# Low weights of 24 feed-forward units made by an accumulating DMA in place of a VectorE subtraction

## The chip, the cores and the metric

The kernel runs on one core of a Trainium2 chip. The metric is the device time of one execution in microseconds, the median over the executions shown. TensorE (PE in the profile) does the matrix products, VectorE (DVE) and ScalarE (ACT) the elementwise work, GpSimd (POOL) little besides constants, and SyncE (SP) issues nearly all weight loads.

## What is computed

A trunk of two layers for 512 prompt frames and 32 sample frames, 544 tokens in all, with a model width of 1024. Around each mixer stand two feed-forward blocks, four in the kernel:

```python
def swiglu(x, w_gu, w_down):
    gate, up = jnp.split(x @ w_gu, 2, axis=-1)
    return (jax.nn.silu(gate) * up) @ w_down
...
def trunk(x, ssm0, conv0, gla0, hgrn0, p):
    ...
    for l in range(DEPTH):
        h = h + 0.5 * swiglu(rms_norm(h, p['norm_ffn1'][l]), p['ffn1_w_gu'][l], p['ffn1_w_down'][l])
        u = rms_norm(h, p['norm_mix'][l])
        ...
        h = h + m
        h = h + 0.5 * swiglu(rms_norm(h, p['norm_ffn2'][l]), p['ffn2_w_gu'][l], p['ffn2_w_down'][l])
```

The hidden width is 2816, that is 22 tiles of 128. Everything is float32.

## The kernel before, in words

**High and low parts.** TensorE is fed float32r operands, which hold fewer bits than float32. Each weight block and each activation is therefore split in two: a high part, the float32r copy, and a low part, the float32r copy of what is left. A product is then three matmuls: high by high, high by low activation, low weight by high activation.

**Units.** A unit is one output tile of 128 rows. Its weights are up to 8 blocks of 128x128 (768 or 1024 columns in a buffer). SyncE loads them into one of four buffers `raw` (`load`); ScalarE copies them to `whi[u % 2]` (`hi`); VectorE subtracts, `raw - whi`, into `wlo[u % 2]` (`lo`); TensorE then multiplies (`unit`, or `unit_rows` for some of its blocks; `row_products` is one block, six matmuls). ScalarE, VectorE, TensorE and SyncE each have an order of their own written out in the code; semaphores tie them: `raw_landed`, `hi_ready`, `lo_ready`, `unit_done`. Since `raw` and `wlo` are reused, SyncE waits with a load for the `lo` of the unit four before, and ScalarE waits with a `hi` for the end of the unit two before.

**The feed-forward blocks.** They are named l0f1, l0f2, l1f1 and l1f2. Each has 8 units for the first four hidden tiles, and then three groups of hidden tiles with 8, 6 and 8 tiles (`GROUPS`). In a group, the gate and up products of most tiles are made by seven partial products each (`product`, p1 to p7, with weights WH and WL); then comes the down projection of the group, 8 units whose block count is the group's tile count: `down0` (8 blocks), `down1` (6 blocks), `down2` (8 blocks).

**Where a down group begins.** TensorE's order is: the last p7 of the group, then blocks 0 and 1 of the first down unit u0, then p3 and p4 of the last hidden tile, then the other blocks of u0, then the units u0+1 to u0+7. TensorE waits for `lo_ready` of u0 before its first matmul, although the low weights are read only by the fifth. ScalarE's order there is: silu of the tile before the last, the copy after p6 of the last tile (`u2_copy`), `hi(u0)`, the copy after p7 (`u3_copy`), one `act_hi`, `hi(u0+1)`, `last_silu`. After that, at the end of each unit u0+j, comes the `hi` of unit u0+j+2. VectorE makes `lo(u0)` and `lo(u0+1)` in the same places, and `lo(u0+j+2)` after the residual of u0+j.

The memory `LR`, `SQ` and `ACC` (one row of 544 numbers each) is used at the ends of blocks and in the mixers, not in down0 and down1.

Of the kernel before, what the change touches and what calls it, by code (L numbers as in the profile page):

```python
# [6 lines left out]
FR = mybir.dt.float32r  # L7
I32 = mybir.dt.int32
ALU = mybir.AluOpType
# [3 lines left out]
P = 128  # L13
# [75 lines left out]
def build(nc, a, o):  # L89
# [3 lines left out]
    with ExitStack() as ctx:  # L93
        def sem(name):
            return ctx.enter_context(nc.semaphore(name))
# [26 lines left out]
        ACC = place("ACC", [T], w)  # L122
        SQ2 = LR
        assert 2 * T >= D
        ident = place("ident", [P], w)
# [123 lines left out]
        end_unit = plan[f"{FFNS[-1][0]}_down{len(GROUPS) - 1}"][0]  # L249

        def kept(u):

            return u >= end_unit + WHOLE
# [5 lines left out]
        def low_of(u):  # L259

            return KW[:, u - end_unit - WHOLE, 1] if kept(u) else wlo[u % 2]

# [86 lines left out]
        def tile(x, m):  # L349
# [5 lines left out]
            xh_ready xl_ready sq_ready acc_done ms_ready rs_ready gate_scaled silu_done act_made ah_ready al_ready  # L355
            lowrank_landed late_rows lb_exp small_landed masks_made row_placed first_tap conv_ready xc_ready z_scaled sz_ready
            dt_in dt_exp dt_plus dt_turned dt_made cum_made rows_psum rows_copied last_rows last_copied last_stored y_summed dct_psum b_turned bt_ready end_diff end_exp cb_psum cb_masked rows_stored lms_landed lm_landed ep_landed lms_ready st_turned lms_masked lm_exp ep_ready
            x_turned xd_made bx_psum hs_ready lm_ready y_psum y_read y_gated y_squared y_mean y_rstd
            y_weighted yh_ready yl_ready h0_psum h0_landed h0_ready hout_copied hout_stored scan_consts_made st_ready gk_psum pre_act forget_made clamped logs_made q_made g_taken far_placed att_ready last_done last_read b_ready e1_ready
# [3 lines left out]
            pair_high pair_low pair_sums product_done pair_copied c22_made parts_high parts_made front_scaled front_silu""".split()  # L363
# [3 lines left out]
        pair_landed = [sem(f"pair_landed{b}") for b in range(2)]  # L367
        y_stored = sem("y_stored")
        passed = {e: sem(f"waits_passed_{e}") for e in ("sp", "pe")}
# [25 lines left out]
        def _(sp):  # L395
            xp = a["x_prompt"].rearrange("b (c t) d -> t (b c) d", t=CH)
            def load(u, slot, src, k, n=P, dst=0):

                hold("sp", S["lo_ready"], u + 1)
                return sp.dma_start(raw[slot][:, 0:k, dst:dst + n], src)  # L400
# [97 lines left out]
            sp.dma_start(DROW[:, :], a["ssm_d"].broadcast_to([P, HA])).then_inc(S["small_landed"], 16)  # L498
            sp.wait_ge(S["late_rows"], 3)
            sp.dma_start(WGK[32:48, :], a["gla_w_gk"][0]).then_inc(S["gate_weights_landed"], 16)  # L500
# [18 lines left out]
            for b in range(2 * KT):  # L519
                col = (COL_XBC, COL_Z)[b % 2] + b // 2 * P  # L520
                load(u0 + b, (u0 + b) % 4, win[:, :, col:col + P], KT).then_inc(raw_landed[(u0 + b) % 4], 16)
                if b == 1:
                    sp.wait_ge(S["rows_stored"], 16)
                    sp.wait_ge(S["late_rows"], 2)
# [56 lines left out]
        def _(pool):  # L581
# [31 lines left out]
            pool.drain().then_inc(S["masks_made"], 1)  # L613

            def scan_consts(m):

                pool.memset(m["rm"][:, :], 1.0)
                pool.memset(m["att"][:, :, :], 0.0)
                pool.memset(m["ac"][:, :, :], 0.0)
                pool.memset(m["vw"][:, :, T:TPAD], 0.0)  # L620
                pool.memset(m["kd"][:, T:TPAD], 0.0)
                pool.memset(m["xl"][:, LV - 2, :], 0.0)
                pool.drain()
                pool.memset(m["rm"][:, 0:T:CH], 0.0)
                pool.drain().then_inc(S["scan_consts_made"], 1)

            pool.wait_ge(S["unit_done"], plan["ab_heads"][0] + CREDIT)
            states_out(pool)
            scan_consts(GM)
            pool.wait_ge(S["rs_ready"], 5)  # L630
            scan_consts(CM)


        @block.scalar
        def _(act):
# [19 lines left out]
            def run(name, evac, begun=False):  # L655
# [14 lines left out]
                for b in range(min(4, n)):  # L670
# [21 lines left out]
            def rms(e, name=None):  # L692

                logs_set()
                if e == 2:
                    act.wait_ge(S["late_rows"], 1)
                    A(LB[:, 1, :], LB[:, 0, :], ACT.Exp).then_inc(S["lb_exp"], 1)
# [90 lines left out]
            def ffn(f, e, name=None, final=False, after_first=None):  # L788
# [25 lines left out]
                for g, nf, ss in groups(f):  # L814
# [6 lines left out]
                    for s in ss:  # L821
# [659 lines left out]
        def _(dve):  # L1481
            TT, STT, TSC = dve.tensor_tensor, dve.scalar_tensor_tensor, dve.tensor_scalar

            def lo(u):

                k = unit_rows[u]
                dve.wait_ge(S["hi_ready"], u + 1)
                TT(low_of(u)[:, 0:k, :], raw[u % 4][:, 0:k, :],  # L1488
                   high_of(u)[:, 0:k, :].bitcast(F), ALU.subtract).then_inc(S["lo_ready"], 1)
# [332 lines left out]
            lo(2)  # L1822
            dve.wait_ge(S["masks_made"], 1)
            ffn(0, 1, begun=True)

            dve.wait_ge(S["early_vec"], 3)
            TT(LB[:, 0, :], vec[:, V_LB:V_LB + KT], vec[:, V_LB:V_LB + KT], ALU.subtract).then_inc(S["late_rows"], 1)
# [3 lines left out]
            dve.drain().then_inc(S["late_rows"], 1)  # L1831
            dve.memset(WGK[0:64, :], 0.0)
            dve.drain().then_inc(S["late_rows"], 1)
# [3 lines left out]
            dve.wait_ge(S["masks_made"], 1)  # L1837
            dve.memset(PM[:, 2, NC * HA:(NC + 1) * HA], 0.0)
# [267 lines left out]
            def heads(name, nh, m, g0, weights, first, t0):  # L2106
# [165 lines left out]
                if not gla:  # L2272
                    pre(0)
                    units(0, 2)
                dve.wait_ge(S["scan_consts_made"], first)
                cumulate(0)
# [198 lines left out]
            for j in range(KT):  # L2475
# [3 lines left out]
                lo(u0 + j + 2)  # L2479
            dve.wait_ge(S["lb_exp"], 1)  # L2480
            dve.reciprocal(LB[:, 2, :], LB[:, 1, :])
# [17 lines left out]
        def _(pe):  # L2499
# [44 lines left out]
            def unit_rows(ps, r0, r1, k, x, before=None):  # L2544

                if r0 == 0:
                    pe.wait_ge(S["lo_ready"], ps + 1 + CREDIT)
                    pe.wait_ge(S["pair_read"], ps - 1 + CREDIT)
# [650 lines left out]
```

## Time and profile before

| | |
|---|---|
| median of 2 runs | 2325.43 us (2325.21 to 2325.66) |
| span of the profiled execution, which is its own time | 2325.5 us |
| TensorE busy | 2294.0 us, 99% |
| VectorE busy | 1720.5 us, 74% |
| ScalarE busy | 1143.9 us, 49% |
| GpSimd busy | 14.4 us, 1% |
| packets of the main load queue, share of 16 DMA engines | 30.7% |

An engine that is busy 99% leaves little to gain by relieving another one. What matters is at which places TensorE's next work is ready only just in time.

### The profile page before, as it was taken

Reading aid. Unit: us, or ns where it says so; the run is one execution under the profiler, and the core shown is the slowest. Engines: PE = TensorE matmul, PEld = TensorE weight load, DVE = VectorE, ACT = ScalarE, POOL = GpSimd, SP = SyncE. Lnnn points to the kernel's source line nnn. Section 1 sums busy time; section 2 is a strip of 40 time slices with the busy share of each in tenths; the row PEclk is TensorE's granted clock in tenths of the full one; section 3 lists DMA queues with packets and bytes.
Section 4 is the critical chain, followed back from the end, with each engine's and each line's share of the span. In section 5 each row is a group of like instructions: output and inputs, shape, how many; then the busy total and the mean of one; then the engine's idle time right before and its main releaser. Section 6 shows DMA issues by size and latency. Waiting matters only on the chain.

```text
span 2325.5 us, 49874 instructions
## 1 busy us (share of the span) xinstructions
PE 2294.0 (99%) x20579; PEld 2266.2 (97%) x20579; DVE 1720.5 (74%) x2587; ACT 1143.9 (49%) x1769; POOL 14.4 (1%) x50
## 2 busy tenths in 40 slices
PE   8999999999999999999999999999999999999998
PEld 8999999999999999999999999999999999999998
DVE  7767876788577567677867767876888867767885
ACT  6434444676354545343445434444677756424453
POOL 1000000000000000000000000000000000000000
PEclk9999999999999999999999999999999999999999
DMA  4323333332422223333323323332222223323331
GB/s 149 105 77 103 94 96 86 94 119 74 121 71 63 76 82 93 98 92 106 95 82 98 111 75 103 95 94 84 70 71 68 69 74 91 96 82 102 88 107 57
DMA packets 397773, 209.92 MB, mean 90 GB/s; under 512 B 11679, under 2 KB 393750, under 8 KB 397558
## 3 DMA queue, kind: packets, MB, share of 16 engines
q1 hardware_dynamic: 392166, 203.17, 30.7%
q10 hardware_dynamic: 5392, 3.72, 0.5%
q8 instruction: 155, 2.54, 0.5%
q14 instruction: 60, 0.49, 0.1%
HBM read 201.41 MB, written 5.45 MB: 89 GB/s over the span
## 4 chain that ended last, share of the span: by engine, by line
PE 83%; DVE 7%; ACT 4%; DVEq 3%; issue 1%; ACTq 1%; DMA 0%; SPq 0%
PE PD L2509 8%; PE PM L2619 8%; PE PM L2617 8%; PE PD L2514 8%; PE PM L2618 8%; PE PD L2515 8%; PE PD L2513 7%; PE PD L2510 7%; PE PD L2516 7%; PE PD L2619 3%; PE PD L2617 3%; PE PD L2618 3%; DVE wlo L1488 1%; DVE c_xl L2199 1%; DVE c_xl L2175 1%
## 5 line engine op out<-in xcount | busy, mean ns | idle before, releaser
L653 ACT ACTIVATE whi<-raw 128x1024 fp32r<-128x1024 f32 (+3 forms) x231 | 229.1, 992 | 356.7 <-PE PD L2516 350.8
L1488 DVE TENSOR_TENSOR wlo<-raw,whi 128x1024 fp32r<-128x1024 f32 (+3 forms) x233 | 267.3, 1147 | 69.3 <-ACT whi L653 47.9
L2509 PE MATMUL PD<-XB,whi 128*128 128x288 f32 x856 | 262.8, 307 | 2.2 <-DVE wlo L1488 2.0
L2514 PE MATMUL PD<-XB,whi 128*128 128x288 f32 x856 | 252.8, 295 | 0.0
L2515 PE MATMUL PD<-XB,wlo 128*128 128x288 f32 x856 | 252.0, 294 | 0.0
L2513 PE MATMUL PD<-XB,whi 128*128 128x256 f32 x856 | 241.9, 283 | 0.3 <-DVE XB L1526 0.3
L2510 PE MATMUL PD<-XB,whi 128*128 128x256 f32 x856 | 240.0, 280 | 0.0
L2516 PE MATMUL PD<-XB,wlo 128*128 128x256 f32 x856 | 238.3, 278 | 0.0
L2619 PE MATMUL PM<-XT,WL 128*128 128x272 f32 x720 | 208.3, 289 | 0.0
L2617 PE MATMUL PM<-XT,WH 128*128 128x272 f32 x720 | 207.6, 288 | 0.0
L2619 PE MATMUL PM<-XB,WL 128*128 128x272 f32 x720 | 207.6, 288 | 0.0
L2617 PE MATMUL PM<-XB,WH 128*128 128x272 f32 x720 | 207.5, 288 | 0.0
L2618 PE MATMUL PM<-XT,WH 128*128 128x272 f32 x720 | 207.1, 288 | 0.0
L2618 PE MATMUL PM<-XB,WH 128*128 128x272 f32 x720 | 207.0, 287 | 0.0
L2509 PE MATMUL PD<-AB,whi 128*128 128x288 f32 x664 | 196.9, 297 | 0.0
L2514 PE MATMUL PD<-AB,whi 128*128 128x288 f32 x664 | 196.4, 296 | 0.0
L2515 PE MATMUL PD<-AB,wlo 128*128 128x288 f32 x664 | 194.6, 293 | 0.0
L2513 PE MATMUL PD<-AB,whi 128*128 128x256 f32 x664 | 188.7, 284 | 0.0
L2510 PE MATMUL PD<-AB,whi 128*128 128x256 f32 x664 | 186.4, 281 | 0.0
L2516 PE MATMUL PD<-AB,wlo 128*128 128x256 f32 x664 | 185.1, 279 | 0.0
L2509 PEld LDWEIGHTS PD<-XB,whi 128*128 128x128 f32 x856 | 161.1, 188 | 5.7 <-issue 2.8
L2515 PEld LDWEIGHTS PD<-XB,wlo 128*128 128x128 f32 x856 | 162.1, 189 | 0.0
(519 smaller groups left out, 6683.7 us busy)
## 6 DMA issues: line engine op xcount, KB each, us to landing
raw<-in_ffn_w_down SPq DMA_DIRECT2D x64, 512.0 KB, 3.8
V<-in_ffn_w_gu SPq DMA_DIRECT2D x60, 512.0 KB, 3.9
V<-in_ffn_w_gu SPq DMA_DIRECT2D x120, 256.0 KB, 4.5
raw<-in_ab_w_in SPq DMA_DIRECT2D x44, 512.0 KB, 3.9
raw<-in_ffn_w_gu SPq DMA_DIRECT2D x32, 512.0 KB, 3.8
raw<-in_c_w_in SPq DMA_DIRECT2D x32, 512.0 KB, 4.0
raw<-in_ffn_w_down SPq DMA_DIRECT2D x32, 384.0 KB, 3.3
VF<-in_ffn_w_gu SPq DMA_DIRECT2D x12, 512.0 KB, 4.6
```

The lines of the kernel that those rows point to most:

```text
L653: A(high_of(ps)[:, 0:k, :], raw[ps % 4][:, 0:k, :], ACT.Copy).then_inc(S["hi_ready"], 1)
L1488: TT(low_of(u)[:, 0:k, :], raw[u % 4][:, 0:k, :], high_of(u)[:, 0:k, :].bitcast(F), ALU.subtract).then_inc(S["lo_ready"], 1)
L2175: TT(xn[:, :, 0, :], mid, bn[:, :, 0, :], ALU.subtract)
L2509: mm(front, hi, x[:, 0, r, 0:FRONT], start=first, stop=False)
L2510: mm(rest, hi, x[:, 0, r, FRONT:T], start=first, stop=False)
L2513: mm(rest, hi, x[:, 1, r, FRONT:T], start=False, stop=False)
L2514: mm(front, hi, x[:, 1, r, 0:FRONT], start=False, stop=False)
L2515: mm(front, lo, x[:, 0, r, 0:FRONT], start=False, stop=final)
L2516: return mm(rest, lo, x[:, 0, r, FRONT:T], start=False, stop=final)
L2617: mm(out, hi, moving[:, 0, q, :], start=q == 0 and opens, stop=False, skip_group_check=not opens)
L2618: mm(out, hi, moving[:, 1, q, :], start=False, stop=False, skip_group_check=not opens)
L2619: last = mm(out, lo, moving[:, 0, q, :], start=False, stop=q == 3, skip_group_check=not opens)
```

## The change

For three units, u0, u0+1 and u0+2, in down0 and down1 of each of the four blocks (24 units), VectorE's subtraction is gone. Instead ScalarE writes the negated high weights into the buffer of the low ones (a second pass over `raw` with scale -1, `negate`), and GpSimd issues a DMA from `raw` to that buffer which adds, so that it then holds `raw - high`. The third low buffer of a group is a new one, NEG, which lies over LR and SQ. TensorE waits for the DMA's semaphore before the unit's first matmul, and SyncE waits for it, not for `lo_ready`, with the load into the same `raw` buffer. VectorE only counts `lo_ready` up. Several semaphores are folded into others with the same meaning, which changes no order.

```diff
+        NEG = at("NEG", [KR, P], w[0] - 3 * 2176, FR)
...
+        by_dma = [plan[f"{tag}_down{g}"][0] + j for tag, _ in FFNS for g in range(2) for j in range(3)]
...
         def low_of(u):
 
+            if u in by_dma and by_dma.index(u) % 3 == 2:
+                return NEG
             return KW[:, u - end_unit - WHOLE, 1] if kept(u) else wlo[u % 2]
...
             def load(u, slot, src, k, n=P, dst=0):
 
-                hold("sp", S["lo_ready"], u + 1)
+                if isinstance(u, int) and u - 4 in by_dma:
+                    q = by_dma.index(u - 4)
+                    sp.wait_ge(dma_low[q % 3], 16 * (q // 3 + 1))
+                else:
+                    hold("sp", S["lo_ready"], u + 1)
                 return sp.dma_start(raw[slot][:, 0:k, dst:dst + n], src)
...
+            def lows(f):
+
+                for n in range(6 * f, 6 * f + 6):
+                    u = by_dma[n]
+                    k = unit_rows[u]
+                    pool.wait_ge(S["negated"], n + 1)
+                    pool.dma_start(low_of(u)[:, 0:k, :], raw[u % 4][:, 0:k, :], accum_op=ALU.add).then_inc(dma_low[n % 3], 16)
+
+            lows(0)
             pool.wait_ge(S["unit_done"], plan["ab_heads"][0] + CREDIT)
             states_out(pool)
             scan_consts(GM)
+            lows(1)
+            lows(2)
             pool.wait_ge(S["rs_ready"], 5)
             scan_consts(CM)
+            lows(3)
...
+            def negate(u):
+
+                k = unit_rows[u]
+                act.wait_ge(raw_landed[u % 4], 16 * (u // 4 + 1))
+                act.wait_ge(S["unit_done"], u - 1 + CREDIT)
+                A(low_of(u)[:, 0:k, :], raw[u % 4][:, 0:k, :], ACT.Copy, scale=-1.0).then_inc(S["negated"], 1)
...
                         else:
                             hi(u0 + 1, 0, nf)
+                            if g < 2:
+                                negate(u0 + 1)
                             last_silu(len(GROUPS) * f + g, s)
                         if s == last - 1:
                             hi(u0, 0, nf)
+                            if g < 2:
+                                negate(u0)
...
                             hi(ahead, 0, unit_rows[ahead])
+                            if ahead in by_dma:
+                                negate(ahead)
...
             def lo(u):
 
+                if u in by_dma:
+                    dve.sem_inc(S["lo_ready"], 1)
+                    return
                 k = unit_rows[u]
...
             def unit_rows(ps, r0, r1, k, x, before=None):
 
                 if r0 == 0:
+                    if ps in by_dma:
+                        pe.wait_ge(dma_low[by_dma.index(ps) % 3], 16 * (by_dma.index(ps) // 3 + 1))
                     pe.wait_ge(S["lo_ready"], ps + 1 + CREDIT)
                     pe.wait_ge(S["pair_read"], ps - 1 + CREDIT)
```

ScalarE at the start of l0f1's down0, first before, then after. `whi` and `raw` carry the number of their buffer; L653 and L675 are `hi`, L703 is `negate`, L739 and L768 `u2_copy`, L746 and L775 `u3_copy`, the row on AB `act_hi`, and the two rows that follow are `last_silu`.

```order
L739 ACTIVATE US<-PM 128x272
L653 ACTIVATE whi_56<-raw_52 128x1024
L746 ACTIVATE US<-PM 128x272
L763 ACTIVATE AB<-AV 128x544
L653 ACTIVATE whi_57<-raw_53 128x1024
L756 ACTIVATE TG<-TG 128x272
L758 ACTIVATE TG<-TG 128x272
L763 ACTIVATE AB<-AV 128x544
L653 ACTIVATE whi_56<-raw_54 128x1024
```

```order
L768 ACTIVATE US<-PM 128x272
L675 ACTIVATE whi_56<-raw_52 128x1024
L703 ACTIVATE wlo_58<-raw_52 128x1024
L775 ACTIVATE US<-PM 128x272
L792 ACTIVATE AB<-AV 128x544
L675 ACTIVATE whi_57<-raw_53 128x1024
L703 ACTIVATE wlo_59<-raw_53 128x1024
L785 ACTIVATE TG<-TG 128x272
L787 ACTIVATE TG<-TG 128x272
L792 ACTIVATE AB<-AV 128x544
L675 ACTIVATE whi_56<-raw_54 128x1024
L703 ACTIVATE NEG<-raw_54 128x1024
```

Each of the three copies to `whi` has a second pass over the same `raw` right behind it; nothing else changed its place.

TensorE at the same place, with the waits of each row, before and after: the last two matmuls of p7 and the first block of u0.

```order
L2618 MATMUL PM<-XB,WH_82 128x272
L2619 MATMUL PM<-XB,WL_83 128x272
L2509 MATMUL PD<-AB,whi_56 128x288 [waits ah_ready,pair_read,lo_ready]
L2510 MATMUL PD<-AB,whi_56 128x256
L2513 MATMUL PD<-AB,whi_56 128x256 [waits al_ready]
L2514 MATMUL PD<-AB,whi_56 128x288
L2515 MATMUL PD<-AB,wlo_58 128x288
```

```order
L2660 MATMUL PM<-XB,WH_83 128x272
L2661 MATMUL PM<-XB,WL_84 128x272
L2547 MATMUL PD<-AB,whi_56 128x288 [waits pair_read,ah_ready,lo_ready,dma_low0]
L2548 MATMUL PD<-AB,whi_56 128x256
L2551 MATMUL PD<-AB,whi_56 128x256 [waits al_ready]
L2552 MATMUL PD<-AB,whi_56 128x288
L2553 MATMUL PD<-AB,wlo_58 128x288
```

The order is the same; the unit's first matmul now waits for the DMA as well.

## Rows read from the trace of the kernel before

**Rows 1.** The page's first part: busy us, share of the span, instructions.
```profile
PE 2294.0 (99%) x20579; PEld 2266.2 (97%) x20579; DVE 1720.5 (74%) x2587; ACT 1143.9 (49%) x1769; POOL 14.4 (1%) x50
```

**Rows 2.** Windows over the eight down starts: busy us (PE, PEld, DVE, ACT, POOL), granted clock.
```profile
96.00:136.00 40.00, 40.00 (x321) 40.00 (x320) 22.30 (x33) 13.22 (x18) 0.00 (x0) 1.00 0.47 132
...
sum 290.00, PE 290.00 PEld 289.47 DVE 166.59 ACT 94.45 POOL 0.00; mean PE 36.25 PEld 36.18 DVE 20.82 ACT 11.81 POOL 0.00
```

**Rows 3.** TensorE's longest-summed wait over the span: us in total, times, longest.
```profile
PE PD L2509 <- DVE wlo L1488: 4.5, 7, 1.5
```

**Rows 4.** Timeline, l0f1 down0, first two units: start us, us, instruction.
```profile
104.12 1.05 ACT L653 ACTIVATE whi<-raw 128x1024 fp32r<-128x1024 f32 x1
107.75 1.04 ACT L653 ACTIVATE whi<-raw 128x1024 fp32r<-128x1024 f32 x1
108.70 0.41 ACT L756 ACTIVATE TG<-TG 128x272 f32<-128x272 f32 x1
110.99 0.43 ACT L758 ACTIVATE TG<-TG 128x272 f32<-128x272 f32 x1 [1.88 <-DVEq L1632]
...
105.20 1.22 DVE L1488 TENSOR_TENSOR wlo<-raw,whi 128x1024 fp32r<-128x1024 f32 x1 [1.98 <-ACT whi L653]
...
106.56 0.32 PE L2509 MATMUL PD<-AB,whi 128*128 128x288 f32 x1
```

**Rows 5.** Timeline, l0f1 down0, third unit.
```profile
115.88 1.06 ACT L653 ACTIVATE whi<-raw 128x1024 fp32r<-128x1024 f32 x1 [3.01 <-PE PD L2516]
...
121.65 0.30 PE L2509 MATMUL PD<-AB,whi 128*128 128x288 f32 x1
```

**Rows 6.** Timeline, l0f1 down1, first and third unit.
```profile
215.60 0.83 ACT L653 ACTIVATE whi<-raw 128x768 fp32r<-128x768 f32 x1
226.02 0.85 ACT L653 ACTIVATE whi<-raw 128x768 fp32r<-128x768 f32 x1 [1.68 <-PE PD L2516]
...
218.06 0.29 PE L2509 MATMUL PD<-AB,whi 128*128 128x288 f32 x1
...
230.24 0.29 PE L2509 MATMUL PD<-AB,whi 128*128 128x288 f32 x1
```

**Rows 7.** The last of the eight places, l1f2 down1, first unit.
```profile
2136.51 0.83 ACT L653 ACTIVATE whi<-raw 128x768 fp32r<-128x768 f32 x1
...
2138.96 0.29 PE L2509 MATMUL PD<-AB,whi 128*128 128x288 f32 x1
```

**Rows 8.** DMA issues: names, queue, count, KB each, median us from issue to landing.
```profile
raw<-in_ffn_w_down SPq DMA_DIRECT2D x64, 512.0 KB, 3.8
raw<-in_ffn_w_down SPq DMA_DIRECT2D x32, 384.0 KB, 3.3
out_y_p<-yout SPq DMA_DIRECT2D x3, 512.0 KB, 2.6
out_gla_p<-g_s ACTq DMA_DIRECT2D x4, 128.0 KB, 1.7
xin<-in_x_prompt SPq DMA_DIRECT2D x4, 512.0 KB, 6.7
```

**Rows 9.** Windows around two drops of the clock (the column behind POOL is the granted clock).
```profile
580.00:583.37 3.37, 1.42 (x6) 0.95 (x7) 3.01 (x5) 2.01 (x5) 0.00 (x0) 1.00 0.15 45
583.37:586.78 3.41, 3.41 (x17) 3.41 (x16) 1.72 (x3) 1.25 (x2) 0.00 (x0) 0.50 0.37 110
...
1941.90:1945.29 3.39, 1.68 (x10) 1.38 (x10) 2.40 (x4) 2.35 (x3) 0.00 (x0) 1.00 0.47 139
1945.29:1948.70 3.41, 3.41 (x15) 3.17 (x14) 2.30 (x3) 3.03 (x4) 0.00 (x0) 0.50 0.06 18
```

**Rows 10.** Timeline of TensorE: the waits before both drops, and one without a drop.
```profile
581.95 1.13 PE L2898 MATMUL PM<-SQY,ones 128*128 128x512 f32 x2 [2.15 <-DVEq L2011]
...
1944.63 1.57 PE L2564 MATMUL PM<-ACC,ones 128*128 128x272 f32 x4 [1.34 <-DVEq L2442]
...
1892.50 0.40 PE L2509 MATMUL PD<-COB,whi 128*128 128x288 f32 x1 [1.48 <-DVE wlo L1488]
```

More of the change, by code:

```diff
@@ L355, in build @@
             xh_ready xl_ready sq_ready acc_done ms_ready rs_ready gate_scaled silu_done act_made ah_ready al_ready
-            lowrank_landed late_rows lb_exp small_landed masks_made row_placed first_tap conv_ready xc_ready z_scaled sz_ready
+            lowrank_landed small_landed row_placed first_tap conv_ready xc_ready z_scaled sz_ready
             dt_in dt_exp dt_plus dt_turned dt_made cum_made rows_psum rows_copied last_rows last_copied last_stored y_summed dct_psum b_turned bt_ready end_diff end_exp cb_psum cb_masked rows_stored lms_landed lm_landed ep_landed lms_ready st_turned lms_masked lm_exp ep_ready
             x_turned xd_made bx_psum hs_ready lm_ready y_psum y_read y_gated y_squared y_mean y_rstd
-            y_weighted yh_ready yl_ready h0_psum h0_landed h0_ready hout_copied hout_stored scan_consts_made st_ready gk_psum pre_act forget_made clamped logs_made q_made g_taken far_placed att_ready last_done last_read b_ready e1_ready
+            y_weighted yh_ready yl_ready h0_psum h0_landed h0_ready hout_copied hout_stored st_ready gk_psum pre_act forget_made clamped logs_made q_made g_taken far_placed att_ready last_done last_read b_ready e1_ready
             kd_exp kd_ready gk_read tree_diff tree_exp tree_made turned turned_read level_psum level_placed
@@ L362, in build @@
             g_scaled gs_ready go_made goh_ready gol_ready squares_added gate_weights_landed step_exp yt_psum yt_copied early_rows first_rows rows_late yf_ready y_col y_rs y_scaled
-            pair_high pair_low pair_sums product_done pair_copied c22_made parts_high parts_made front_scaled front_silu""".split()
+            negated pair_high pair_low pair_sums product_done pair_copied c22_made parts_high parts_made front_scaled front_silu""".split()
         S = {n: sem(n) for n in names}
@@ L367, in build @@
         pair_landed = [sem(f"pair_landed{b}") for b in range(2)]
+        dma_low = [sem(f"dma_low{b}") for b in range(3)]
         y_stored = sem("y_stored")
@@ L498, in _ @@
             sp.dma_start(DROW[:, :], a["ssm_d"].broadcast_to([P, HA])).then_inc(S["small_landed"], 16)
-            sp.wait_ge(S["late_rows"], 3)
+            sp.wait_ge(S["early_rows"], 5)
             sp.dma_start(WGK[32:48, :], a["gla_w_gk"][0]).then_inc(S["gate_weights_landed"], 16)
@@ L523, in _ @@
                     sp.wait_ge(S["rows_stored"], 16)
-                    sp.wait_ge(S["late_rows"], 2)
+                    sp.wait_ge(S["early_rows"], 4)
                     decay_rows(0)
@@ L612, in _ @@
                 pool.tensor_copy(MASK[32 * g:32 * g + 32, 5, :], ident[32 * g:32 * g + 32, 32 * g:32 * g + 32])
-            pool.drain().then_inc(S["masks_made"], 1)
+            pool.drain().then_inc(S["consts_made"], 1)
             def scan_consts(m):
@@ L624, in scan_consts @@
                 pool.memset(m["rm"][:, 0:T:CH], 0.0)
-                pool.drain().then_inc(S["scan_consts_made"], 1)
+                pool.drain().then_inc(S["consts_made"], 1)
+            def lows(f):
[5 more added lines that the diff above has]
+            lows(0)
             pool.wait_ge(S["unit_done"], plan["ab_heads"][0] + CREDIT)
@@ L695, in rms @@
                 if e == 2:
-                    act.wait_ge(S["late_rows"], 1)
-                    A(LB[:, 1, :], LB[:, 0, :], ACT.Exp).then_inc(S["lb_exp"], 1)
+                    act.wait_ge(S["early_rows"], 3)
+                    A(LB[:, 1, :], LB[:, 0, :], ACT.Exp).then_inc(S["dt_exp"], 1)
                 if name:
@@ L1822, in _ @@
             lo(2)
-            dve.wait_ge(S["masks_made"], 1)
+            dve.wait_ge(S["consts_made"], 3)
             ffn(0, 1, begun=True)
             dve.wait_ge(S["early_vec"], 3)
-            TT(LB[:, 0, :], vec[:, V_LB:V_LB + KT], vec[:, V_LB:V_LB + KT], ALU.subtract).then_inc(S["late_rows"], 1)
+            TT(LB[:, 0, :], vec[:, V_LB:V_LB + KT], vec[:, V_LB:V_LB + KT], ALU.subtract).then_inc(S["early_rows"], 1)
             dve.memset(LMS[:, :, :], 0.0)
@@ L1830, in _ @@
             dve.memset(BT[:, NC, :, :], 0.0)
-            dve.drain().then_inc(S["late_rows"], 1)
+            dve.drain().then_inc(S["early_rows"], 1)
             dve.memset(WGK[0:64, :], 0.0)
-            dve.drain().then_inc(S["late_rows"], 1)
+            dve.drain().then_inc(S["early_rows"], 1)
             dve.memset(XLAST[:, :], 0.0)
@@ L1836, in _ @@
             dve.memset(XE[1][:, 0:3], 0.0)
-            dve.wait_ge(S["masks_made"], 1)
+            dve.wait_ge(S["consts_made"], 3)
             dve.memset(PM[:, 2, NC * HA:(NC + 1) * HA], 0.0)
@@ L2274, in heads @@
                     units(0, 2)
-                dve.wait_ge(S["scan_consts_made"], first)
+                dve.wait_ge(S["consts_made"], 3 + first)
                 cumulate(0)
@@ L2479, in _ @@
                 lo(u0 + j + 2)
-            dve.wait_ge(S["lb_exp"], 1)
+            dve.wait_ge(S["dt_exp"], 3)
             dve.reciprocal(LB[:, 2, :], LB[:, 1, :])
@@ L2546, in unit_rows @@
                 if r0 == 0:
+                    if ps in by_dma:
+                        pe.wait_ge(dma_low[by_dma.index(ps) % 3], 16 * (by_dma.index(ps) // 3 + 1))
                     pe.wait_ge(S["lo_ready"], ps + 1 + CREDIT)
```

## Prediction

> **What bounds the kernel now.** The first thing to read is the page's busy line: TensorE is busy 99% of the span, VectorE 74%, ScalarE 49% [rows 1]. The change relieves VectorE, so the next question is whether TensorE waits for VectorE where the change is made. The view by windows answers it: over the eight stretches in which down0 and down1 begin, 290 us together, TensorE is busy all 290.00 us at the full granted clock [rows 2]. The list of TensorE's waits names the subtraction that the change removes only 7 times, 4.5 us in all [rows 3], and since nothing is idle in those eight windows, all of that is elsewhere. So no time can be gained at these places; the question is what can be lost, and that is read from how early each low block is ready.
>
> The timeline shows it. At the start of l0f1's down0 ScalarE begins the high copy of u0 at 104.12, VectorE's subtraction runs from 105.20 to 106.42, and TensorE begins u0 at 106.56 [rows 4]. The subtraction is ready 0.14 us ahead, no more. It can't start earlier, since ScalarE's order puts the high copy behind the copy that follows p6. For u0+2 the copy begins at 115.88, once u0 is finished, and TensorE wants the unit at 121.65 [rows 5]. In down1, with units a quarter shorter, the two distances are 215.60 to 218.06 and 226.02 to 230.24 [rows 6]. The first distance is 2.44 to 2.46 us at all eight places; the last of them is 2136.51 to 2138.96 [rows 7]. TensorE has no slack there of its own, so each microsecond that a low block comes late is a microsecond of the end.
>
> **The change, part by part.**
>
> *VectorE's 24 subtractions go.* 24 times at most 1.22 us [rows 4] is at most 29 us of VectorE time. TensorE waits for none of it in the eight windows [rows 2], so this is worth 0.
>
> *ScalarE gets 24 second passes.* A pass has the size of the high copy, 1.05 us (8 blocks) or 0.83 us (6 blocks), and ScalarE starts its next operation 0.95 us after such a copy's start (107.75 and 108.70) [rows 4]. It is on the path of the low weights, but what else is queued behind it has cover. Behind the pass for u0 stands the copy after p7, which can't start before p7 ends at 106.56, when the pass is over (106.12, below). Behind the pass for u0+1 stands the last silu; ScalarE idled 1.88 us before its second half at 110.99 [rows 4], which takes in the 1.05 us. Behind the pass for u0+2 ScalarE has nothing for microseconds. Cost of its own: 0.
>
> *The path of the low weights now is: high copy, negated copy, semaphore to GpSimd, DMA, semaphore to TensorE.* Let D be the time from the end of the negated copy to the DMA's landing, GpSimd's issue included. In down0, u0: the negated copy ends at 104.12 + 0.95 + 1.05 = 106.12, TensorE wants the unit at 106.56, so it waits D - 0.44. u0+2: 115.88 + 2.00 = 117.88 against 121.65, so it waits D - 3.77. In down1, u0: 215.60 + 0.73 + 0.83 = 217.16 against 218.06: D - 0.90. u0+2: 226.02 + 1.58 = 227.60 against 230.24: D - 2.64. Unit u0+1 costs nothing: its negated copy ends at 107.75 + 2.00 = 109.75 and TensorE wants it when u0 is done, which is when the copy at 115.88 starts [rows 5], and later still by what u0 waited. A wait of u0 does not eat the wait of u0+2, because the high copy of u0+2 waits for the end of u0 and moves with it.
>
> *What D is.* No DMA in this trace is issued by GpSimd, goes from SBUF to SBUF, or adds. The nearest rows: a store of the same 512 KB out of SBUF, with runs as long, lands in 2.6 us, one of 128 KB in 1.7 us; so 384 KB by the line between them is 2.3 us [rows 8]. An adding DMA has to read its destination as well, before it writes. The lower end is that this is free: D = 2.6 and 2.3. The upper end is two whole landings of the weight loads of these sizes, 3.8 and 3.3 us: D = 7.6 and 6.6 [rows 8]. I take two trips of the store, D = 5.2 and 4.6, since the store is the nearer row in its source and its run length, and the second read and GpSimd's issue are both to be paid from the second trip.
>
> The sum at that value: down0 4.76 + 1.43 = 6.19, down1 3.70 + 1.96 = 5.66, together 11.85 us per feed-forward block, and 47.4 us for the four.
>
> The Trainium skill speaks to the same number. Its page "Collectives: The Full Stack", section "The bandwidth ceiling: the fold count and why AG ≠ RS ≠ AR", says that an adding transfer is slower because it needs two source reads, not because of the add; its page "DMA: Bandwidth & Descriptors", section "Anatomy of one DMA — SWDGE (gpsimd) path", gives for a DMA issued from GpSimd about 2.0 us plus the bytes over 436 GB/s. With the bytes counted twice that would be 4.4 and 3.8 us, and the sum 34.6 us before any effect on the clock. No run here shows either yet.
>
> *The clock.* Twice in this trace the granted clock fell to 0.50, half of 2.4 GHz, for 3.41 us: behind a wait of TensorE of 2.15 us at 581.95 and behind one of 1.34 us at 1944.63, in a stretch with other gaps [rows 9, 10]. A wait of 1.48 us at 1892.50 left it alone [rows 10]. 3.41 us at half the clock lose 1.7 us of work. The waits of u0 (4.8 and 3.7 us) are longer than any of these, so I count a drop for all 8; the waits of u0+2 (1.4 and 2.0 us) lie between the rows, so I count one for half of them. 12 times 1.7 us is 20.5 us; the bounds are 0 and 16 times 1.7, 27.3 us.
>
> *The load queue.* SyncE now waits for the DMA of u0 with the load of u0+4, so that load starts some 5 us later, and behind it stand u0+5 and the first pair load of the next group. The load takes 3.8 us [rows 8]. A unit takes TensorE some 6 us, so u0+4 is wanted 12 us after u0+2, 27 us after u0 [rows 4, 5]. This is covered. So is the traffic: the DMA engines are busy 0.47 of the time in the first window [rows 2], and u0's DMA starts when the loads of u0 to u0+3 have landed. The folded semaphores are worth 0: they are counted at the same points. GpSimd is idle nearly always [rows 1], and its constants for the mixers stand between the groups' DMAs, not ahead of one that is due.
>
> Sum: 47.4 + 20.5 = 67.9 us on the profiled execution's 2325.5 us, which stands at the median of the runs (2325.43). **Forecast: 2393 us.**
>
> **The rivals.**
>
> *The DMA is short (not slower by 2%).* If reading the destination costs nothing and GpSimd's issue is quick, D is 2.6 and 2.3: waits of 2.16 us in down0 and 1.40 in down1 for u0, none for u0+2, 14.2 us in all and no drop of the clock: 2340 us. For it speaks the share of the DMA engines that is free; against it that two reads and a write of the bytes are needed. From D of about 4.3 and 3.8 on (33.8 us of waits and 8 drops, 13.6 us) the change is 2% slower, and below that it is not. A change of 2%, 46.5 us, is about what a measurement of this kernel can tell from none.
>
> *VectorE's relief pays (a little faster).* The only waits on the removed kind of instruction are 4.5 us [rows 3], none here. Even if all went, the time would be 2321 us. It needs D under 0.44, and the shortest landing in the rows is 1.7 us [rows 8].
>
> *The DMA is long.* GpSimd issues no DMA in this trace, so its issue may take long, and the destination has another number type than the source. The slowest landing of 512 KB in the trace, with other transfers in the way, is 6.7 us [rows 8]; two such trips, 13.4 and some 12 us, give waits of 13.0 + 9.6 + 11.1 + 9.4 = 43.1 us per block, 172 us, and with 27 us for the clock 2525 us. At D = 7.6 and 6.6 it would be 82.6 + 27.3, 2435 us.
>
> *The change does less than it says.* If TensorE did not really wait for the DMA, the time would stay at 2325 us; the order of the changed kernel shows the wait on the unit's first matmul, so this has next to no chance.
>
> **How the numbers follow.** I give the forecast's case (D between 4.3 and about 8) 0.60, the short DMA 0.20, the long one 0.17, a gain or no effect 0.03. The range reaches from just above the short end, 2345, to just above the two-load bound, 2445 us; it leaves out the long case and the lowest part of the short one. Slower by over 2% takes the first and third case, 0.77; within 2% the second and most of the last, 0.21; faster by over 2% keeps 0.02, since all of TensorE's waits for the removed instruction are 0.2% of the time.
>
> **What the changed kernel's profile would show.** TensorE idle before the first matmul of u0 at eight places, by 4 to 5 us, ended by a DMA out of `raw`; before u0+2 by 1 to 2 us; never before u0+1. The median landing of the new DMAs at 4 to 5 us. The granted clock at 0.50 for about 3.4 us behind each long wait. VectorE's busy time lower by under 29 us, ScalarE's higher by some 23 us, TensorE's longer by the slow stretches alone. The forecast is wrong if D is outside 4.3 to 8, if the high copy of u0 runs earlier than 2.4 us ahead of TensorE's need, or if the clock holds through the waits, which would leave 2373 us.

## The result, and the profile after

| | before | after |
|---|---|---|
| median | 2325.43 us | 2384.63 us (2384.51 to 2384.75, 2 runs) |
| ratio | | 1.0251, 95% interval 1.0221 to 1.0281 |
| span of the profiled execution | 2325.5 us | 2382.8 us |

The change makes the kernel 59.2 us slower. The forecast was 2393 us, with a range of 2345 to 2445. The spans lie 57.3 us apart. The changed kernel's time is 1.7 us above its span (2384.51 and 2382.8 us), and so it is in every run with both numbers; by that the profiled execution of the kernel before, with its span of 2325.5 us, took some 2327.2 us and was neither of the two timed ones. Its later executions, 47 in three sets, have medians of 2326.02 to 2327.85 us, so the loss is rather 57 us than 59. One execution among the experiments below, of the run in which VectorE adds, took 3161.57 us at a mean granted clock of 0.65 and is not counted.

The page's first part of the changed kernel, against [rows 1]:

```profile
PE 2313.1 (97%) x20579; PEld 2280.9 (96%) x20579; DVE 1696.4 (71%) x2563; ACT 1163.4 (49%) x1793; POOL 34.8 (1%) x74
```

VectorE has lost 24.1 us of work and ScalarE has gained 19.5 us, as the change means them to. TensorE makes the same 20579 matmuls and is yet busy 19.1 us longer; the rest of the 57.3 us of span is idle time. Both parts have to be found.

TensorE's waits over the span (us in total, times, longest), against [rows 3]:

```profile
PE PD L2547 <- DMA wlo<-raw: 30.6, 8, 4.4
PE PD L2547 <- DMA NEG<-raw: 9.2, 8, 1.4
PE PD L2547 <- DVE wlo L1526: 5.9, 7, 2.8
```

Of the three units of a group two have a wait each: 8 waits of 30.6 us for the first unit (u0), 8 of 9.2 us for the third (u0+2, the buffer NEG). The second never waits. The waits on VectorE, outside these groups, are as many as before; one of them is 2.83 us long in place of 1.48 us [rows 10].

The timeline shows how one wait comes about: l0f1's down0, u0, against [rows 4]. ScalarE's high copy, its negated copy, GpSimd's issue, TensorE's first matmul:

```profile
103.98 1.05 ACT L675 ACTIVATE whi<-raw 128x1024 fp32r<-128x1024 f32 x1
104.92 1.05 ACT L703 ACTIVATE wlo<-raw 128x1024 fp32r<-128x1024 f32 x1
...
106.29 1.00 POOL L643 DMA_DIRECT2D wlo<-raw  x1 [93.75 <-ACT wlo L703]
...
110.99 0.61 PE L2547 MATMUL PD<-AB,whi 128*128 128x288 f32 x1 [4.40 <-DMA wlo<-raw]
```

The negated copy ends at 105.97. TensorE would have begun at 106.59 and begins at 110.99, 5.0 us after the copy's end. The same place in down1, and the two third units:

```profile
229.26 0.61 PE L2547 MATMUL PD<-AB,whi 128*128 128x288 f32 x1 [3.31 <-DMA wlo<-raw]
...
129.24 0.40 PE L2547 MATMUL PD<-AB,whi 128*128 128x288 f32 x1 [0.87 <-DMA NEG<-raw]
...
245.72 0.40 PE L2547 MATMUL PD<-AB,whi 128*128 128x288 f32 x1 [1.41 <-DMA NEG<-raw]
```

GpSimd's DMA rows, from the view of its line (duration of the issue in ns, min/median/max; below, time to landing):

```profile
L643 POOL DMA_DIRECT2D wlo<-raw x16: 851/866/1002, 106.3 to 2192.3; - x16
L643 POOL DMA_DIRECT2D NEG<-raw x8: 851/862/882, 124.7 to 2204.4; - x8
...
DMA to landing us min/median/max: 3.8/4.5/6.5
```

TensorE's longer busy time is mostly the clock. Four of the eight stretches at half clock, one of each length in each kind of group, and the sum over all eight (columns as in [rows 9]):

```profile
108.74:115.57 6.83, 4.58 (x20) 4.58 (x21) 0.00 (x0) 1.03 (x2) 0.87 (x1) 0.50 0.92 160
228.21:235.04 6.83, 5.78 (x25) 5.78 (x26) 0.00 (x0) 0.49 (x2) 0.86 (x1) 0.50 0.69 133
...
1361.43:1364.85 3.42, 2.83 (x12) 2.83 (x13) 0.00 (x0) 0.00 (x0) 0.47 (x1) 0.50 0.79 123
1480.90:1484.31 3.41, 3.41 (x17) 3.41 (x16) 0.00 (x0) 0.00 (x0) 0.00 (x0) 0.50 0.99 220
...
sum 40.97, PE 34.04 PEld 34.05 DVE 0.26 ACT 2.61 POOL 3.93; mean PE 4.26 PEld 4.26 DVE 0.03 ACT 0.33 POOL 0.49
```

Each begins during or behind a wait for u0. In them TensorE works for 34.0 us at half its clock; half of that, 17.0 us, is an upper figure for the loss, since the busy time also holds TensorE's slow start behind the wait. The run with filled waits, below, gives 15.1 us. It also gives what the list of waits leaves out, some 0.3 us for each of the 16 waits, 4.5 us. The two drops of [rows 9] did not come in this execution, which gives 3.4 us back; they come in some of the runs below and not in others, whatever the edit. The longer wait on VectorE takes 1.4 us. So 39.8 + 15.1 + 4.5 - 3.4 + 1.4 = 57.4 us stand against 57.3 us of span.

### The profile page after: what moved, and what is told of

It reads as the page before. It is cut to its first block, busy times and chain, and to the rows that moved or that the text cites. A ratio compares the mean times of both kernels' runs of the same rounds, so it can differ in the third digit from the quotient of the medians.

```text
span 2382.8 us, 49946 instructions
## 1 busy us (share of the span) xinstructions
PE 2313.1 (97%) x20579; PEld 2280.9 (96%) x20579; DVE 1696.4 (71%) x2563; ACT 1163.4 (49%) x1793; POOL 34.8 (1%) x74
## 3 DMA queue, kind: packets, MB, share of 16 engines
q1 hardware_dynamic: 392166, 203.17, 30.2%
## 4 chain that ended last, share of the span: by engine, by line
PE 75%; DVE 9%; ACT 5%; DVEq 4%; issue 3%; DMA 3%; ACTq 1%; POOL 0%; POOLq 0%
PE PD L2547 7%; PE PM L2659 7%; PE PM L2661 7%; PE PM L2660 7%; PE PD L2552 7%; PE PD L2553 7%; PE PD L2551 6%; PE PD L2548 6%; PE PD L2554 6%; PE PD L2661 3%; PE PD L2659 3%; PE PD L2660 3%; DVE wlo L1526 2%; DMA NEG<-raw 1%; DMA wlo<-raw 1%
## 5 line engine op out<-in xcount | busy, mean ns | idle before, releaser
L675 ACT ACTIVATE whi<-raw 128x1024 fp32r<-128x1024 f32 (+3 forms) x231 | 229.1, 992 | 360.4 <-PE PD L2554 354.6
L1526 DVE TENSOR_TENSOR wlo<-raw,whi 128x1024 fp32r<-128x1024 f32 (+3 forms) x209 | 241.2, 1154 | 52.2 <-ACT whi L675 31.5
L2547 PE MATMUL PD<-AB,whi 128*128 128x288 f32 x664 | 200.9, 303 | 39.8 <-DMA wlo<-raw 30.6
L2552 PE MATMUL PD<-AB,whi 128*128 128x288 f32 x664 | 198.7, 299 | 0.0
L2553 PE MATMUL PD<-AB,wlo 128*128 128x288 f32 x608 | 180.3, 297 | 0.0
L2554 PE MATMUL PD<-AB,wlo 128*128 128x256 f32 x608 | 171.8, 283 | 0.0
L2547 PEld LDWEIGHTS PD<-AB,whi 128*128 128x128 f32 x664 | 126.3, 190 | 43.3 <-DMA wlo<-raw 32.4
```

The source lines that it names most:

```text
L675: A(high_of(ps)[:, 0:k, :], raw[ps % 4][:, 0:k, :], ACT.Copy).then_inc(S["hi_ready"], 1)
L1526: TT(low_of(u)[:, 0:k, :], raw[u % 4][:, 0:k, :], high_of(u)[:, 0:k, :].bitcast(F), ALU.subtract).then_inc(S["lo_ready"], 1)
L2547: mm(front, hi, x[:, 0, r, 0:FRONT], start=first, stop=False)
L2552: mm(front, hi, x[:, 1, r, 0:FRONT], start=False, stop=False)
L2553: mm(front, lo, x[:, 0, r, 0:FRONT], start=False, stop=final)
L2554: return mm(rest, lo, x[:, 0, r, FRONT:T], start=False, stop=final)
```

## Experiments

Theory 1 is the prediction's: only the distance between the landing of the low block and TensorE's need counts, and the clock follows TensorE's idleness. The rivals: ScalarE's second passes, the load queue or the DMA traffic cost something of their own; each of the 24 units costs about the same; the clock falls for another reason; the landing is long for another reason than the adding. The times of each set of runs go with their own runs of the kernel before (2327.48, 2327.85 and 2326.02 us for the first four, the second four and the last two).

### One unit at a time

The list of units is cut to those with j = 1, 0 or 2; the others are VectorE's again.

```diff
-        by_dma = [plan[f"{tag}_down{g}"][0] + j for tag, _ in FFNS for g in range(2) for j in range(3)]
+        every = [plan[f"{tag}_down{g}"][0] + j for tag, _ in FFNS for g in range(2) for j in range(3)]
+        by_dma = [u for n, u in enumerate(every) if n % 3 in (1,)]
```

Second unit only:

> Of the change only u0+1 of each group stays with the DMA (8 units); u0 and u0+2 are back with VectorE. The second pass stands ahead of the last silu, and the DMA has 6 us in down0 and 4.5 us more than that path in down1. Theory 1: its low weights land after about 5.3 us (5.0 in down1), 109.8 + 5.3 = 115.1 against a need at 115.6 in down0, so a wait of 0 to 0.5 us at most, no drop of the clock: the time of the kernel before, within 3 us. Rival, that each of the 24 units costs about the same (57 us / 24 = 2.4 us): plus 19 us.

First unit only:

> Only u0 of each group by DMA (8 units). Theory 1: all waits of u0 (30.6 us) and the clock drops, which in the changed kernel all begin at u0, stay: plus 30.6 and 15 to 18 us, 46 to 49 us over the kernel before. Rival, equal cost for each unit: plus 19 us.

Third unit only:

> Only u0+2 of each group by DMA, into NEG (8 units). Theory 1: the waits of u0+2 alone, 9.2 us, and no drop of the clock, since in the changed kernel none began behind such a wait: plus 9 to 10 us. The prediction's count of a drop behind half of them would give plus 16 us; equal cost for each unit plus 19 us.

| unit by DMA | median | over the kernel before | ratio | waits for the DMA |
|---|---|---|---|---|
| u0+1 | 2327.26 us | -0.6 us | 0.9998 (0.9988 to 1.0008) | none |
| u0 | 2371.68 us | 43.8 us | 1.0183 (1.0166 to 1.0200) | 30.2 us |
| u0+2 | 2338.36 us | 10.5 us | 1.0045 (1.0029 to 1.0062) | 9.1 us |

Their waits for the DMA, from the lists of waits of the runs of u0 and of u0+2:

```profile
PE PD L2550 <- DMA wlo<-raw: 30.2, 8, 4.4
```
```profile
PE PD L2550 <- DMA NEG<-raw: 9.1, 8, 1.4
```

The rival of equal cost falls: the same DMA costs 0, 44 or 10 us by its place. The second pass and the DMA of u0+1 are free. The first unit came out a little under its forecast of 46 to 49 us. For the third unit the waits alone account for 9.1 of the 10.5 us, and no stretch at half clock begins in a group.

### TensorE's order: the low products last

In the 24 units TensorE makes the products with high weights for all blocks first, and waits for the low weights only then.

```diff
+                if ps in by_dma:
+                    if r0 == 0:
+                        pe.wait_ge(S["hi_ready"], ps + 1)
+                        pe.wait_ge(S["pair_read"], ps - 1 + CREDIT)
+                    for r in range(r0, r1):
+                        high_block(ps, r, x, before and (lambda p: before(p, r)))
+                    if r1 == k:
+                        low_blocks(ps, k, x)
+                    return
```

`high_block` is `row_products` without its last two matmuls; `low_blocks` waits for the low weights and makes those two for every block.

> Everything of the change stays (second passes, DMAs, traffic), but in the 24 units TensorE makes all products with high weights first and waits for the DMA only before those with low weights. Theory 1, that only TensorE's wait for the landing costs: the low weights are then wanted 56 matmuls of 0.125 us, 7.0 us, after the start of u0 in down0 (6.0 us in down1) and 4.0 and 3.0 us after that of u0+2; they land 4.4, 3.3, 0.9 and 1.4 us after it. All waits and all drops of the clock go: 2325 us, within 3. Rival, that the extra ScalarE passes, the load queue or the DMA traffic carry part of the loss: at least 10 us stay, 2335 us or more.

2332.63 us, ratio 1.0021 (1.0012 to 1.0031), that is 5.1 us over the kernel before. All DMAs and second passes are there, and of the 16 waits for a DMA one of 0.5 us is left. TensorE's waits from 100 to 240 us, in l0f1, the block that has it:

```profile
PE PD L2577 <- DMA NEG<-raw: 0.5, 1, 0.5
PE PD L2567 <- DVE AB L1696: 0.2, 1, 0.2
PE PD L2563 <- ACT AB L792: 0.2, 1, 0.2
```

Over 50 us of the 59 are gone, so what costs is TensorE's wait. But the forecast of 2325 us, within 3, was missed, and the rest could be either the new order or the DMAs. The control gives the same order to the kernel before, with VectorE's subtractions:

> Control for the run with the low products last: the kernel before, VectorE's subtractions and all, with the same new order of TensorE's products in the same 24 units. If the 4 to 5 us that the run with the DMAs kept over the kernel before come from the new order of the matmuls, this kernel shows them too: 2330 us or so beside 2327. If they come from the DMAs or ScalarE's second passes, this one stays at the time of the kernel before, within 1 us.

2333.47 us, ratio 1.0021 (1.0012 to 1.0031), 5.6 us over. The rest is the order's, not the DMA's. TensorE makes the first high products of a group in less time and comes sooner to what waits for the last hidden tile; the control shows such waits where the kernel before has none (from 100 to 240 us):

```profile
PE PD L2531 <- DVE AB L1660: 0.2, 1, 0.2
PE PD L2527 <- ACT AB L765: 0.2, 1, 0.2
```

The list shows 0.4 us of it; the starts of the matmuls show all. In down1 of l0f1, u0 begins at 218.06 in the kernel before [rows 6] and at 218.42 in the control, and u0+1 begins, first before, then in the control:

```profile
225.76 0.29 PE L2509 MATMUL PD<-AB,whi 128*128 128x288 f32 x1
```
```profile
227.17 0.30 PE L2527 MATMUL PD<-AB,whi 128*128 128x288 f32 x1
```

So u0 takes 8.75 in place of 7.70 us there, and in down0 9.39 in place of 9.06 us. The other three blocks show the same to within 0.02 us, and four times 1.05 + 0.33 us is 5.5 us: the new order costs its time in the first units, whose blocks stand between the products of the last hidden tile.

### Idle matmuls in the waits

```diff
+            def keep_busy(ps, before=None):
+                n = by_dma.index(ps)
+                count = ((30, 0, 5), (22, 0, 9))[n // 3 % 2][n % 3]
...
+                for _ in range(count):
+                    mm(line(ps)[:, 0:FRONT], high_of(ps)[:, 0, :], AB[:, 0, 0, 0:FRONT], start=True, stop=True)
```

> The changed kernel, with idle matmuls put where TensorE waits for the DMA: 30 before u0 in down0, 22 in down1, 5 and 9 before u0+2, each 288 columns and 0.125 us, into the bank that the unit then overwrites. The wait stays as long, but TensorE isn't idle. Theory 1 says that the loss is 39.8 us of waits and some 17 to 19 us of half clock that follows from the idleness: the clock stays at full and the time is 2366 us, within 4. Rival, that the clock falls for another reason or that the loss beside the waits is something else: it stays at 2383 us.

2377.59 us, ratio 1.0215 (1.0198 to 1.0232), 50.1 us over its runs of the kernel before, where 40.6 were forecast. The clock did what theory 1 says. l0f1's down0 with its filled wait, and the stretch behind it:

```profile
107.40:112.10 4.70, 4.28 (x33) 4.04 (x31) 1.17 (x2) 3.16 (x5) 1.79 (x2) 1.00 0.59 112
112.10:116.00 3.90, 3.90 (x31) 3.90 (x32) 0.56 (x2) 0.00 (x0) 0.00 (x0) 1.00 0.99 142
```

The granted clock stays at 1.00 there and in all eight groups, though TensorE's own work stands still just as long. So the drops follow from idleness. The time was missed all the same. TensorE's busy time in this run is 2333.7 us, 39.7 us more than in the kernel before, and these waits are left:

```profile
PE PD L2547 <- DMA wlo<-raw: 3.7, 8, 1.0
PE PD L2547 <- DMA NEG<-raw: 3.4, 8, 0.9
```

39.7 and 7.1 are 46.8 us, against waits of 39.8 in the changed kernel. The filling wasn't too long: at all 16 places TensorE's own first matmul starts 0.04 us after the landing of its DMA, as in the changed kernel. The forecast left out two things. First, a wait costs more than the list says, as l0f1's u0 shows:

```profile
112.03 0.40 PE L2547 MATMUL PD<-AB,whi 128*128 128x288 f32 x1 [0.42 <-DMA wlo<-raw]
112.27 0.28 PE L2548 MATMUL PD<-AB,whi 128*128 128x256 f32 x1
```

The second matmul starts 0.24 us after the first and not 0.13 us as in dense work, and the last matmul before a wait is counted as busy to its end, 0.29 us after its start, where the next could start after 0.13 us. That is some 0.3 us for each wait, in the changed kernel too, 4.5 us for 16. Second, four of the DMAs landed 0.3 to 0.7 us later than in the changed kernel, 2.3 us together; why is open. With the 39.8 us these make 46.6 us. The profiled span, 2372.8 us, is 2325.5 and 46.8 us to within 0.5 us; the timed median lies higher, since the profiled execution, 2374.51 us, is the fastest of four that reach up to 2379.0 us.

This run also tells what the clock cost. From the start of u0 to the start of u0+1 the changed kernel takes 11.19 us in the first group and the filled one 9.16 us; over the eight groups it is 83.0 and 67.9 us. The difference of 15.1 us is the loss by the clock.

### The path: the order of ScalarE's two copies, and VectorE in the DMA's place

The negated copy goes first:

```diff
                         if s == last - 1:
-                            hi(u0, 0, nf)
                             if g < 2:
                                 negate(u0)
+                            hi(u0, 0, nf)
```

and so at the two other places. TensorE and the load into the same `raw` also wait for `hi_ready`, since the high copy now ends last.

> The changed kernel with the negated copy ahead of the high copy in all 24 units, so that the DMA starts one pass earlier. Theory 1, the length of the path sets the wait: every wait is shorter by 0.95 us (down0) and 0.75 us (down1): 3.45, 2.55, 0 and 0.65 us, 26.6 us in all in place of 39.8. With 8 drops of the clock left the time is 2365 to 2371 us. Rival, that the DMA starts no earlier or is held by something else (GpSimd's issue, the queue): 2384 us.

2374.73 us, ratio 1.0202 (1.0185 to 1.0219), 47.3 us over, where 40 to 46 were forecast. Its waits:

```profile
PE PD L2548 <- DMA wlo<-raw: 27.2, 8, 5.2
...
PE PD L2548 <- DMA NEG<-raw: 3.2, 6, 0.7
```

30.4 us in place of 39.8: the waits became shorter, so the DMA was held by ScalarE's passes and not by GpSimd, but 3.8 us less so than forecast. Six of the eight first waits are 2.5 to 3.6 us, as forecast; two are 5.2 and 4.8 us, since their DMAs landed 6.4 and 6.1 us after the issue instead of 4.6. These two alone of the eight were issued while the last of the group's four weight loads was still in flight (105.56 us against its landing at 105.91, 2061.26 against 2062.21). That this is the cause isn't shown: in the run with filled waits a DMA issued 0.6 us before such a landing took 4.55 us.

VectorE adds `raw` onto the negated high weights:

```diff
+                if u in by_dma:
+                    dve.wait_ge(S["negated"], by_dma.index(u) + 1)
+                    TT(low_of(u)[:, 0:k, :], raw[u % 4][:, 0:k, :],
+                       low_of(u)[:, 0:k, :].bitcast(F), ALU.add).then_inc(S["lo_ready"], 1)
+                    return
```

> The second passes of ScalarE stay, but VectorE adds raw onto the negated high weights in place of the DMA, so the path is longer than before by one pass alone. Theory 1: the low block is ready 1.05 (0.83) us later than in the kernel before, whose margins were 0.14 us in down0 and about 0.65 us in down1, so TensorE waits some 0.8 and 0.2 us at u0 and nowhere else: 4 us in all, no drop of the clock, 2329 us. Rival, that ScalarE's second passes are a main cost (they delay the copies and silus behind them): 2345 us or more.

2332.53 us without the one execution named above, ratio 1.0020 (1.0010 to 1.0030), 5.1 us over, where 4 was forecast. The waits at u0 of down0 are as forecast; those of down1, 0.2 us each in the forecast, are too short for the list:

```profile
PE PD L2541 <- DVE wlo L1516: 2.8, 4, 0.7
```

The starts of the matmuls show TensorE fall back by 0.9 us at u0 in each down0 and by 0.3 us in each down1, 5.1 us in all. So 24 second passes cost little, and only through the longer path ahead of u0; what remains of the 59 us, some 54, comes by difference with the DMA: its time, and the clock that falls behind the waits.

### Does the adding make the landing long?

```diff
-                    pool.dma_start(low_of(u)[:, 0:k, :], raw[u % 4][:, 0:k, :], accum_op=ALU.add).then_inc(dma_low[n % 3], 16)
+                    pool.dma_start(low_of(u)[:, 0:k, :], raw[u % 4][:, 0:k, :]).then_inc(dma_low[n % 3], 16)
```

> The changed kernel with a plain copy of raw into the low buffers in place of the adding DMA: same bytes written, same queue, same places, but the destination isn't read and the subtraction is left out of the result for these 24 units. The changed kernel's landings are 4.6 us for 512 KB and 3.95 us for 384 KB, 0.65 us more for 128 KB, so 2.6 us of the 4.6 grow with the size. If the adding costs a second reading of the bytes, half of that goes: 3.3 us and 2.95 us, waits of 3.1, 2.3, 0 and 0.4 us in place of 4.4, 3.3, 0.9 and 1.4, 23 us in all in place of 39.8, and 2360 to 2367 us. Rival, that GpSimd's issue and fixed costs are what is long: landings and time as in the changed kernel, 2384 us.

2360.45 us, ratio 1.0142 (1.0125 to 1.0158), within the forecast. GpSimd's rows and the landings:

```profile
L643 POOL DMA_DIRECT2D wlo<-raw x16: 537/537/680, 106.6 to 2172.8; - x16
L643 POOL DMA_DIRECT2D NEG<-raw x8: 537/537/547, 121.4 to 2183.5; - x8
...
DMA to landing us min/median/max: 2.6/2.9/6.3
```

The median landing falls from 4.5 to 2.9 us and GpSimd's issue from 0.86 to 0.54 us; TensorE's waits for it are 20.3 us in all, where 23 were forecast. By size, the DMAs for u0 and u0+2 landed after 4.4 to 4.7 us (512 KB) and 3.8 to 4.0 us (384 KB) with the adding, and after 2.9 to 3.0 and 2.6 us without it, but for one of each size with 3.7 and 3.8 us. So the adding costs about 1.6 us of a landing of 512 KB and 1.3 us of one of 384 KB; the plain copy itself still costs TensorE half of the waits, since it starts so late.

### The same DMA, started earlier

u0 and u0+1 by DMA, u0+2 with VectorE, and ScalarE's two copies of u0 moved ahead of a silu before which it sat idle:

```diff
-                        if s == last - 1:
-                            hi(u0, 0, nf)
-                            if u0 in by_dma:
-                                negate(u0)
...
+                        if s == last - 1:
+                            hi(u0, 0, nf)
+                            if u0 in by_dma:
+                                negate(u0)
                         if s < last:
                             silu(hidden_of(s), s % 2)
```

> u0 and u0+1 by DMA, u0+2 back with VectorE, and ScalarE's high and negated copies of u0 moved ahead, in front of the silu before which ScalarE sat idle 4.8 us in down0 (5.1 us in down1). Theory 1, that only the distance between the DMA's start and TensorE's need counts: in l0f1 and l1f2, where the weights land at 100.6 of 106.6, the low block of down0 lands at 100.6 + 2.0 + 5.0 = 107.6, a wait of 1.0 us; elsewhere none. Plus 2 to 4 us in place of the 44 us of u0 alone: 2330 us. Rival, that the DMA needs its 4.4 us of TensorE's time wherever it starts, or that the moved copies delay the copies and silus behind them: 2340 us or more.

2333.04 us, ratio 1.0033 (1.0020 to 1.0045), 7.0 us over, where 2 to 4 were forecast and u0 alone in its old place had cost 44. ScalarE's copies as they now stand in l0f1, and TensorE's first matmul of u0:

```profile
100.41 1.06 ACT L678 ACTIVATE whi<-raw 128x1024 fp32r<-128x1024 f32 x1 [2.15 <-DMA raw<-in_ffn_w_down]
101.37 1.04 ACT L706 ACTIVATE wlo<-raw 128x1024 fp32r<-128x1024 f32 x1
103.08 0.66 ACT L783 ACTIVATE TG<-TG 128x544 f32<-128x544 f32 x1 [0.67 <-DVEq L1673]
...
108.18 0.41 PE L2550 MATMUL PD<-AB,whi 128*128 128x288 f32 x1 [1.64 <-DMA wlo<-raw]
```

The silu still waits for VectorE, so the copies are covered. Now the weights' own landing from HBM is what the high copy waits for. The DMA, issued at 102.73 us with two weight loads still in flight, landed after 5.4 us in place of 4.7 us, and makes the wait 1.6 us where 1.0 was forecast. The waits for the DMA are 3.8 us in three places, in l0f1 and l1f2, where the weights land late; the other five are gone:

```profile
PE PD L2550 <- DMA wlo<-raw: 3.8, 3, 1.7
```

The profiled span is 3.7 us over that of the kernel before, as these waits say; the timed medians are 7 us apart. The profiled execution, 2330.89 us, is the fastest of six that reach up to 2334.84 us; what else makes up the 3 us is open. No version is faster than the kernel before beyond its interval.

## Why the prediction was right

**What bounds the kernel.** Right. TensorE had no slack at the eight places, nothing was won by VectorE's 24.1 us less, and the time is lost where the low weights come late.

**What costs nothing.** Right for ScalarE's passes on the engine itself (the run of u0+1 alone: ratio 0.9998), for the load queue and the traffic (the low products last, against its control: 2332.63 and 2333.47 us), and for the second unit. The loads of 512 KB from `in_ffn_w_down` did land later, at the median 4.9 us after their issue in place of 3.8 us, but TensorE did not wait for them. ScalarE gained 19.5 us and not some 23, as a second pass starts 0.94 us after the first (103.98 and 104.92), before that has ended.

**The time D.** This is the term that carried the sum, and its size was slightly high. Forecast 5.2 and 4.6 us; the first DMA of down0 landed 106.29 + 4.66 - 105.97 = 5.0 us after the negated copy, the first of down1 4.3 us. The waits were 4.4, 3.3, 0.9 and 1.4 us against a forecast of 4.8, 3.7, 1.4 and 2.0: 39.8 in place of 47.4 us. The way to D, two trips of a plain store, was lucky in part. The trace of the kernel before has another store of the same tile and size, issued by ScalarE, that landed in 3.8 us; two such trips would have made D 7.6 us. The plain copy without the adding landed in 2.9 us for 512 KB, near the store's 2.6 us [rows 8]; the adding put 1.6 us on it and not another 2.6; and the semaphore and GpSimd's start, 0.3 us (105.97 to 106.29), had no term of their own. The estimate from the Trainium skill's pages was 4.4 and 3.8 us, with 34.6 us of waits: "Collectives: The Full Stack", section "The bandwidth ceiling: the fold count and why AG ≠ RS ≠ AR", gives the two source reads of an adding transfer, there for ReduceScatter, and "DMA: Bandwidth & Descriptors", section "Anatomy of one DMA — SWDGE (gpsimd) path", the 2.0 us plus the bytes over 436 GB/s. The trace comes out a little above that rule: a landing of 4.66 and 3.96 us from the issue, and 39.8 us of waits.

**The clock.** Right in mechanism: the filled waits show it. Wrong in its count, and near in its sum partly by chance. I counted 12 drops of 3.41 us, 20.5 us. There were 8, none behind the waits of u0+2 (0.9 and 1.4 us), and four of the eight lasted 6.83 us instead of 3.41; TensorE lost 15.1 us in them. "Twice in this trace" was also a miscount: a third drop begins at 2320.75 us, behind TensorE's last matmul, and costs nothing.

**The sum.** 67.9 us forecast, 59.2 us measured and 57.3 us between the spans: 7.6 us too much for the waits and 5.4 us too much for the clock; nothing for TensorE's stop and start around each wait, which cost 4.5 us; and 2.0 us less outside the groups (the two drops that did not come, the longer wait on VectorE). The errors have both signs and cancel in part. The short DMA (D under 4.3 and 3.8 us) was the nearest rival, and D stood 0.7 and 0.5 us from that point. The long one had more chance than it deserved.

## What to carry to other kernels

Before moving work from a busy engine to a path that takes longer, look at the distance between the start of that path and the need of the engine that bounds the kernel: the same DMA cost 0, 10 or 44 us by place alone, and relief of an engine that the bounding one doesn't wait for is worth nothing. A wait of a few microseconds on TensorE costs more than its length, since its clock can drop behind it; here 39.8 us of waits brought 15.1 us more by the clock and 4.5 us more at their edges. Where such a path must be used, start it in an idle stretch ahead or put other work of TensorE before the need; both took most of the loss away.

## What the runs showed of the hardware

In the changed kernel an adding DMA of 512 KB from SBUF to SBUF issued by GpSimd, for u0 or u0+2, landed 4.4 to 4.7 us after its issue and one of 384 KB after 3.8 to 4.0 us. Those of the second units, which run beside the first's DMA and a weight load, took 4.9 to 6.5 us; with the second units' DMAs alone in the kernel it was 4.5 to 4.7 us and 3.9 us. Its issue took GpSimd 0.86 us, that of the plain copy 0.54 us.

The granted clock fell to half at each of the eight waits of 3.3 to 4.4 us, for 3.41 or 6.83 us; it held through all waits of 0.9 to 1.4 us before u0+2, and through the longer ones while they were filled with idle matmuls. I had expected one length. The length of a single wait doesn't decide it: in the run without the adding the clock fell at six of the eight waits before u0, three of them of 1.9 us, and held at one of 2.8 us and one of 1.9 us; in the changed kernel it held behind the wait of 2.83 us at 1936.43 us.

The order of the same matmuls inside 24 units was worth 5.6 us in the control, without any other change, and 5.5 us of it lay in the eight first units.
